# The first layer's output projection, second turn: seven products for eight, with the mixes on GpSimd and VectorE

## The reference

```python
o_p = sb_prompt(qkv[:, :, 0], qkv[:, :, 1], qkv[:, :, 2], sb_bias[i])
xp = xp + o_p.reshape(b, s, -1) @ w_o_a[i]
...
xs = xs + o_s.reshape(db, t, -1) @ w_o_a[i]
```

## Time and profile before

| | us |
|---|---|
| median of 3 executions | 1331.81 |
| lowest, highest | 1331.24, 1335.96 |
| the profiled execution | 1335.28 |
| its span | 1333.4 |
| TensorE busy | 1253.0 (94%) |
| VectorE busy | 629.5 (47%) |
| GpSimd busy | 495.7 (37%) |
| ScalarE busy | 404.2 (30%) |

### The profile page before, as it was taken

How to read it: one execution, slowest core, us unless ns; L and a number is a source line. 1 busy time by engine, 2 the same in 40 slices (tenths; PEclk the granted TensorE clock), 3 DMA queues, 4 the chain that set the end, 5 groups by cost and what they waited for, 6 DMA issues and landing times. The chain is left out here.

```text
span 1333.4 us, 21502 instructions
## 1 busy us (share of the span) xinstructions
PE 1253.0 (94%) x8796; PEld 881.1 (66%) x8796; DVE 629.5 (47%) x1026; ACT 404.2 (30%) x847; POOL 495.7 (37%) x415
## 2 busy tenths in 40 slices
PE   8999999999999998879999999999998989998887
PEld 6787887645666664436969868878756656664443
DVE  3478784623622221256357749648546562221123
ACT  2222422312122221155325526426015312221112
POOL 4456655100111111012986686686630101111102
PEclk8999999999999999999999999999998999999999
DMA  8446645477899999981111112013231899999998
GB/s 316 143 143 200 214 146 174 146 298 312 326 420 418 418 418 418 419 330 48 51 57 58 59 57 96 13 57 99 64 89 35 328 366 420 418 418 418 418 419 315
DMA packets 93317, 318.81 MB, mean 239 GB/s; under 512 B 32457, under 2 KB 44889, under 8 KB 68132
## 3 DMA queue, kind: packets, MB, share of 16 engines
q1 hardware_dynamic: 78500, 279.88, 54.2%
q0 software_dynamic: 13536, 33.29, 7.0%
q10 hardware_dynamic: 1184, 4.26, 0.8%
HBM read 300.06 MB, written 33.34 MB: 250 GB/s over the span
## 5 line engine op out<-in xcount | busy, mean ns | idle before, releaser
L1229 PE MATMUL ps<-slots,oT 128*64 128x256 f32 x1088 | 147.8, 384 | 18.7 <-DMA slots<-in_w_up 9.4
L1255 DVE TENSOR_TENSOR sg<-sg,ps 64x256 f32<-64x256 f32 x64 | 26.5, 413 | 236.3 <-ACT sg L1252 236.3
L1229 PEld LDWEIGHTS ps<-slots,oT 128*64 128x64 f32 x1088 | 100.5, 138 | 56.7 <-issue 18.1
L1756 POOL DMA_INDIRECT xs<-xn_rows,idx x30 | 30.8, 1026 | 235.5 <-PE ps L1218 177.0
L2136 PE MATMUL ps<-slots 128*128 128x384 f32 x320 | 107.2, 489 | 1.5 <-DVE vo L2534 1.5
L1252 ACT ACTIVATE sg<-ps 64x256 f32<-64x256 f32 x64 | 24.4, 381 | 231.4 <-PE ps L1229 231.4
L1762 POOL DMA_INDIRECT y_rows<-ysb,idx x30 | 30.2, 1008 | 166.8 <-DVE ysb L1264 162.3
L2136 PEld LDWEIGHTS ps<-slots 128*128 128x128 f32 x320 | 67.1, 214 | 34.4 <-issue 3.4
L1264 DVE COPY ysb<-ps 64x512 f32<-64x512 f32 x60 | 41.6, 694 | 85.8 <-PE ps L1247 81.1
L610 PE MATMUL ps<-xnT_a,wA 128*128 128x260 f32 (+1 forms) x320 | 77.0, 397 | 1.5 <-DVE xnT_a L874 1.4
L2457 ACT ACTIVATE slots<-slots,neg 128x128 f32<-128x128 f32 (+1 forms) x192 | 64.1, 417 | 43.3 <-DVE neg L2639 43.3
(11 more groups left out here) (384 smaller groups left out, 2664.0 us busy)
## 6 DMA issues: line engine op xcount, KB each, us to landing
slots<-in_w_gate SPq DMA_DIRECT2D x40, 1024.0 KB, 28.2
slots<-in_w_down SPq DMA_DIRECT2D x38, 1024.0 KB, 26.2
slots<-in_w_up SPq DMA_DIRECT2D x28, 1024.0 KB, 25.7
slots<-in_unit_weights_b SPq DMA_DIRECT2D x12, 1536.0 KB, 6.7
wA<-in_qkv_pairs_a SPq DMA_DIRECT2D x24, 512.0 KB, 3.3
spare<-in_w_up SPq DMA_DIRECT2D x12, 1024.0 KB, 29.2
apart<-in_w_gate SPq DMA_DIRECT2D x8, 1024.0 KB, 22.3
apart<-in_w_up SPq DMA_DIRECT2D x8, 1024.0 KB, 23.7
```

The lines of the kernel that those rows point to most:

```text
L1229: last = nc.tensor.matmul(bank(q)[lo:lo + CAP, 0:FE], x[:, k, :], wt[k], start=(k == 0), stop=(k == KT - 1))
```

## The change

Turn 1 is computed by a new class, `SevenProducts`, in place of 8 calls of `product` and `add`. The four tiles of tokens are two systems of two tiles each. In a system the pairs 0, 1 and 2, 3 are the two halves of the sum over pairs, and the two column halves of w_o the other side: a 2 x 2 by 2 x 2 block product, which Strassen's scheme does in 7 block products (table `SEVEN`) instead of 8. Its left operands are, for five of the seven, a sum or difference of two blocks of oT (`LEFT`, 128x256 each), its right operands, for five of the seven, a sum or difference of two blocks of w_o (`RIGHT`, 128x1024 each). Each product is added to or taken from one or two tiles of x. Pair 7 stays alone: its four tile products ride in products 3 and 4, which have one target, and in two products of their own, so a system has 9 products and 14 sums.

The five left mixes of a system are made by VectorE into `kv_tok`; those of the first system stand before its copies of the sample heads, those of the second between its sums. The five right mixes, which both systems use, are made once by GpSimd, behind its last mask, into `apart` (four) and qkvT (one). Banks 5, 6 and 7 are used in turn. The two expert pieces for `apart` are now issued when product 12 (the last that reads a right mix in apart) is done. ScalarE's squares wait for all sums of a system, and all stand behind its two copies of the sample rows; their junk buffer is now the one of the sample tokens' weights. `plan` and the counters keep the semaphores' counts for turns of any number of products and sums.

```diff
+        SEVEN = ((("s", 0), ("t", 0), ((0, 0, 1), (1, 1, 1))),
+                 ((0, 0), ("t", 1), ((0, 1, 1), (1, 1, 1))),
+                 ((1, 1), ("t", 2), ((0, 0, 1), (1, 0, 1))),
+                 (("s", 1), ("t", 3), ((1, 1, 1),)),
+                 (("s", 2), ("t", 4), ((0, 0, 1),)),
+                 (("s", 3), (0, 0), ((1, 0, 1), (1, 1, -1))),
+                 (("s", 4), (1, 1), ((0, 0, -1), (0, 1, 1))))
+        LEFT = (((0, 0), (1, 1), 1), ((1, 0), (0, 0), -1), ((0, 1), (1, 1), -1), ((1, 0), (1, 1), 1), ((0, 0), (0, 1), 1))
+        RIGHT = (((0, 0), (1, 1), 1), ((0, 1), (1, 1), -1), ((1, 0), (0, 0), -1), ((0, 0), (0, 1), 1), ((1, 0), (1, 1), 1))
...
+            def mix_left(self, dve, system, n):
+                if system:
+                    dve.wait_ge(self.proj.s_done, self.done([i for i, (a, _, _) in enumerate(SEVEN) if a == ("s", n)][0]))
+                (ta, ha), (tb, hb), sign = LEFT[n]
+                nc.vector.tensor_tensor(self.left[:, n], self.block(2 * system + ta, ha), self.block(2 * system + tb, hb),
+                                        ALU.add if sign > 0 else ALU.subtract).then_inc(self.s_left, 1)
+
+            def mix_right(self, eng, n, source):
+                (ha, na), (hb, nb), sign = RIGHT[n]
+                eng.tensor_tensor(self.right[n], source(ha, na), source(hb, nb), ALU.add if sign > 0 else ALU.subtract).then_inc(self.s_right, 1)
+
+            def product(self, pe, k):
+
+                system, i = k // self.per, k % self.per
+                out = bank(self.banks[k % len(self.banks)])
+                if k == 0:
+                    pe.wait_ge(self.proj.s_in[self.turn], 16 * len(self.proj.turns[self.turn]))
+                if k >= len(self.banks):
+                    pe.wait_ge(self.proj.s_added, self.added(k - len(self.banks)))
+                elif self.proj.added_before[self.turn]:
+                    pe.wait_ge(self.proj.s_added, self.proj.added_before[self.turn])
...
+                    for j in range(len(self.halves[0])):
+                        terms.append((self.left[:, a[1], j] if a[0] == "s" else self.tokens(self.halves[a[1]][j], 2 * system + a[0]),
+                                      self.right[b[1]][:, j] if b[0] == "t" else self.weights(self.halves[b[0]][j], b[1])))
+                if len(self.targets[i]) == 1:
+                    tile, n, _ = self.targets[i][0]
+                    terms += [(self.tokens(m, 2 * system + tile), self.weights(m, n)) for m in self.alone]
...
+            def add(self, dve, k):
+
+                system, i = k // self.per, k % self.per
+                dve.wait_ge(self.proj.s_done, self.done(k))
+                for j, (tile, n, sign) in enumerate(self.targets[i]):
+                    earlier = [e for e in range(i) for target in self.targets[e] if target[:2] == (tile, n)]
+                    if earlier:
+                        dve.wait_ge(self.proj.s_added, self.added(self.per * system + earlier[-1]))
...
                 load_first(sp, 0, range(NHOME))
+                sp.wait_ge(out_a.s_done, seven.done(seven.per + 3))
                 load_first(sp, 0, APART)
...
-                out_a.product(pe, 1, 0)
-                out_a.product(pe, 1, 1)
+                for k in range(4):
+                    seven.product(pe, k)
...
                 def square(t):
-                    act.wait_ge(out_a.s_added, out_a.added(t))
+                    act.wait_ge(out_a.s_added, seven.system_added(t // 2))
                     norm.square(act, t, junk)
 
-                square(0)
                 act.wait_ge(s_op, 1)
...
-                for t in range(1, NT - 2):
+                for t in range(NT - 2):
                     square(t)
...
+                dve.wait_ge(s_kvo, 64 * NPAIR)
+                for n in range(5):
+                    seven.mix_left(dve, 0, n)
                 for q in range(2):
                     dve.wait_ge(s_pv, q + 1)
...
+                pool.wait_ge(out_a.s_in[1], 16 * len(out_a.turns[1]))
+                pool.wait_ge(s_qk, 2 * NPAIR)
+                wo = flat(xnT)[:, 0:D * NPAIR // 2].rearrange("p (h k n) -> p h k n", h=2, k=2)
+                for n in range(5):
+                    seven.mix_right(nc.gpsimd, n, lambda half, cols: wo[:, half, :, 512 * cols:512 * cols + 512])
                 pool.drain()
                 for t in range(NT - 2):
                     norm.power(pool, t)
```

More of the change, by code:

```diff
@@ L282, in __init__, with plan @@
                 self.s_done, self.s_added = sem(f"oproj_done_{name}"), sem(f"x_added_{name}")
-                self.total = 2 * (NT - 1) * len(turns)
+                self.done_before, self.added_before = [0], [0]
+                for k in range(len(turns)):
+                    self.plan(k, 2 * (NT - 1), 2 * (NT - 1))
+            def plan(self, turn, products, sums):
+                del self.done_before[turn + 1:], self.added_before[turn + 1:]
+                self.done_before.append(self.done_before[turn] + products)
+                self.added_before.append(self.added_before[turn] + sums)
+                self.total = self.added_before[-1]
             def load(self, sp, turn, pairs):
@@ L290, in product @@
                 t, n = i // 2, i % 2
-                k, pairs = 2 * (NT - 1) * turn + i, self.turns[turn]
+                pairs, added = self.turns[turn], self.added_before[turn] + i - 1
                 if i == 0:
                     pe.wait_ge(self.s_in[turn], 16 * len(pairs))
-                if k >= 2:
-                    pe.wait_ge(self.s_added, k - 1)
+                if added > 0:
+                    pe.wait_ge(self.s_added, added)
                 for m in pairs:
@@ new lines, in build, with __init__, tokens, weights @@
+        LEFT = (((0, 0), (1, 1), 1), ((1, 0), (0, 0), -1), ((0, 1), (1, 1), -1), ((1, 0), (1, 1), 1), ((0, 0), (0, 1), 1))
+        RIGHT = (((0, 0), (1, 1), 1), ((0, 1), (1, 1), -1), ((1, 0), (0, 0), -1), ((0, 0), (0, 1), 1), ((1, 0), (1, 1), 1))
+        class SevenProducts:
+            def __init__(self, name, proj, turn, halves, alone, left, right, banks):
+                self.proj, self.turn, self.halves, self.alone, self.left, self.right, self.banks = proj, turn, halves, alone, left, right, banks
+                self.targets = [targets for _, _, targets in SEVEN] + ([((0, 1, 1),), ((1, 0, 1),)] if alone else [])
+                self.per = len(self.targets)
+                self.sums = sum(len(targets) for targets in self.targets)
+                self.s_left, self.s_right = sem(f"left_mixed_{name}"), sem(f"right_mixed_{name}")
+                proj.plan(turn, 2 * self.per, 2 * self.sums)
+            def tokens(self, m, tile):
+                return oT[:, m, 128 * tile:128 * tile + 128]
+            def weights(self, m, n):
+                return self.proj.w[m][:, 512 * n:512 * n + 512]
+            def block(self, tile, half):
+                ms = self.halves[half]
+                return oT[:, ms[0]:ms[-1] + 1, 128 * tile:128 * tile + 128]
+            def done(self, k):
+                return self.proj.done_before[self.turn] + k + 1
+            def added(self, k):
+                i = k % self.per
+                return self.proj.added_before[self.turn] + k // self.per * self.sums + sum(len(t) for t in self.targets[:i + 1])
+            def mix_left(self, dve, system, n):
[16 more added lines that the diff above has]
+                    pe.wait_ge(self.proj.s_added, self.proj.added_before[self.turn])
+                terms = []
+                if i < len(SEVEN):
+                    a, b, _ = SEVEN[i]
+                    if a[0] == "s":
+                        pe.wait_ge(self.s_left, len(LEFT) * system + a[1] + 1)
+                    if b[0] == "t":
+                        pe.wait_ge(self.s_right, b[1] + 1)
+                    for j in range(len(self.halves[0])):
[4 more added lines that the diff above has]
+                    terms += [(self.tokens(m, 2 * system + tile), self.weights(m, n)) for m in self.alone]
+                for j, (a, b) in enumerate(terms):
+                    last = nc.tensor.matmul(out, a, b, start=(j == 0), stop=(j == len(terms) - 1))
+                last.then_inc(self.proj.s_done, 1)
+            def add(self, dve, k):
[5 more added lines that the diff above has]
+                        dve.wait_ge(self.proj.s_added, self.added(self.per * system + earlier[-1]))
+                    elif self.proj.added_before[self.turn]:
+                        dve.wait_ge(self.proj.s_added, self.proj.added_before[self.turn])
+                    xh = x[:, 2 * system + tile, 512 * n:512 * n + 512]
+                    nc.vector.tensor_tensor(xh, xh, bank(self.banks[k % len(self.banks)]),
+                                            ALU.add if sign > 0 else ALU.subtract).then_inc(self.proj.s_added, 1)
+            def system_added(self, system):
+                return self.added(self.per * system + self.per - 1)
@@ L464, in build @@
```

(10 more changed lines are left out.)

23 lines of the change are left out of this document (14 added, 9 removed).

## The result

The changed kernel takes 1345.22 us (median of 4, 1343.31 to 1347.40), the kernel before 1331.76 (4 runs on the same chip); the ratio is 1.0093, 95% interval [1.0071, 1.0115]: **slower by some 12.4 us**. Forecast were 1335.7 and a range of 1330 to 1340.5. The profiled execution took 1343.31, span 1341.4.

A forecast was written before the change was run, and what follows sets the result against it. TensorE, busy 94% of the span, was taken as the bound. Products -3.43, tail +1.5 and taking turns +5.9 were summed as +3.9 us on the median 1331.81: forecast 1335.7, range 1330 to 1340.5.

The forecast's parts named there:

- Products: Second turn on TensorE: 36 matmuls instead of 40, -3.43 us, with no product stalled by a sum.
- Loads: Two apart pieces issued late, at about 321 us, still land before the boundary; cost 0.
- The shift: Experts' stage: its full DMA stream and all that follows move with the stage boundary at 328.68.
- Taking turns: First turn: GpSimd's right mixes and VectorE's SBUF instructions hold each other in turn, delaying TensorE's product 6 by +5.9 us.
- The first wait: First turn: TensorE waits for the first sum behind VectorE's held head 0 product, restarting +1.67 us later.
- The bound of 11: Upper bound of the taking-turns term, whose lower bound was 0 and whose taken value was 5.9 us.
- rival 3: First turn: GpSimd runs all five mixes without giving way and VectorE waits; +9.2 us, 1341.0, chance 0.08.
- Rivals 1 to 3: Mixes: 1, turns cost TensorE nothing (1329.9, chance 0.12); 2, only first 128x1279 product caught (1331.5, 0.10); 3, see rival 3.
- Tail: From second turn's last product to next stage: later sums +0.22, GpSimd's power +0.89, semaphore clearing 0.4; +1.5 us, bounds 1.1 and 1.9.
- what the change does to the time is what it does to the start of the next stage: Stage boundary at 328.68: everything behind it was taken to move by the same amount, with no further cost.
- The two terms that make TensorE wait: Taking turns in the first turn (+5.9 us) and the tail before the boundary (+1.5 us).

The follow-up runs named there:

- a_late: Changed kernel with GpSimd's right mixes begun only when VectorE's last 128x1279 product is done; 1342.01 us, ratio 1.0067.
- b_gap: Kernel before, with only the last square (tile 2) made to wait for all prompt sums; 1340.74 us, ratio 1.0073.
- b_gapbusy: b_gap with three matmuls that nobody reads in TensorE's idle time before the stage boundary; 1338.16 us, ratio 1.0032.
- a_tail: Changed kernel with products that end tile 0 put first and GpSimd's semaphore clearing before its last two powers; 1337.26 us, ratio 1.0034.
- a_busy: Changed kernel with three 128x512 matmuls on nothing at TensorE's end of the stage; 1344.05 us, ratio 1.0091.
- b_mixes: Kernel before plus only the five right mixes on GpSimd, read by nobody, with loads into apart waiting for them; 1340.0 us, ratio 1.0062.
- c_busy: c_so with one more matmul on nothing at TensorE's end of the stage; 1331.29 us, ratio 0.9989.
- a_half: Changed kernel with each right mix cut into two of 128x512; one execution at 1343.21 us.
- a_late_tt: a_late with VectorE's two-input sample-token instruction split into a one-input maximum and a two-input sum; one execution at 1342.11 us.
- c_so: a_tail with the right mixes begun only behind VectorE's last two-input instruction of the first turn; 1330.35 us, ratio 0.9989.

## Why the prediction was wrong

- **Products, right.** Forecast -3.43, measured -3.44, and no second-turn product waited for a sum.
- **Loads, right.** The apart pieces were issued at 319.26 and 319.63 (forecast about 321), and from the first expert matmul to the last expert's gates the time is the same to 0.1 us (to the next stage's first matmul 219.02 us, before 220.60). The shift is kept, also right.
- **Taking turns, right as a mechanism, short by 2.1 us in size.** Product 6 of the first turn started 6.2 us later against the turn's own start (forecast 5.9). The first wait grew by 1.97 (forecast 1.67); the slow product behind it cost nothing more, since product 6 waited for VectorE anyway. What was missing is the product behind the second wait, 4.50 instead of 2.84: 1.7 of the 2.1. With it the past values came 8.04 us later. The bound of 11 covered the total, but it was drawn from rival 3, not from the clock. Rivals 1 to 3 are out in the changed kernel: every two-input instruction beside the mixes was held, none over more than one mix at a time. In a_late, rival 3's mechanism did appear.
- **Tail, +1.5 forecast, +1.9 measured**, the upper bound. GpSimd's power comes 0.9 behind VectorE, as worked out; clearing 15 semaphores takes more than the 0.4 taken: from the power's end at 330.03 to 331.10 there are 1.07 us, and 0.33 of them also passed before, behind the last step (328.35 to 328.68), so about 0.7, an estimate. b_gap's trace gives the same (1.08 from the power's end to the boundary).
- **The step that failed: "what the change does to the time is what it does to the start of the next stage".** It held for the experts and not for what lies between, the routing. The two terms that make TensorE wait were priced at the length of the wait alone. The idle gap before the boundary grew from 0.46 to 2.36 us, the clock fell to 1.2 GHz, and routing took 38.07 us instead of 30.40: 7.7 us with no term, bound or rival. b_gap shows this alone (+7.4), b_gapbusy and a_tail take it away in their traces. With 7.7 and 1.7 for the clock the sum would have been 3.9 + 9.4 = 13.3. (The prediction's three terms as printed add up to 3.97, not 3.9; nothing hangs on it.)

The trace of before had the signs. TensorE's granted clock was 1.00 in the second turn and 0.94 at 540 to 570, where it is busy for 25.95 of 30 us: idle time and clock stood in one row. And the routing, which the prediction took as a stage that only shifts, had a short stretch at the low level of its own:

```profile
340.30:343.50 3.20, 3.20 (x14) 1.54 (x11) 2.79 (x15) 0.00 (x0) 0.00 (x0) 0.50 1.00 422
```

The Trainium skill ("TensorE: Matmul & The Clock Gate", section "Part 1: The HAM clock gate") says that the array's clock follows how busy TensorE has been recently; by that rule a gap can cost more than itself. The changed kernel and b_gap agree (7.7 and 7.4 us behind gaps of 2.36 and 2.09); the stretch just shown had no idle time of TensorE ahead of it since the boundary, so idle time is not all there is to it.

## What to carry to other kernels

Where a change lets TensorE stand idle, price the gap twice: its length, and what the stage behind it would lose if the clock falls; a stage of 30 us paid 7.7 us for 1.9 us more of gap. A saving of a few matmuls counts only if the chain behind the last of them (sum, square, power, clearing) is no longer than before, so order the products such that the last ones feed only the shortest chain. Before you give an "idle" GpSimd a row of long SBUF instructions, look at what VectorE does beside it and who waits for that.

## What the runs showed of the hardware that was not expected

- **Not every gap is followed by a fall, and not every fall has a gap ahead.** Idle gaps of TensorE of 0.46, 0.99 and 1.00 us before the boundary, and of 1.15 (a_busy) and 1.44 us in the first turn, left the clock up; those of 2.09, 2.32, 2.36, 2.45, 3.41 and 5.07 us were followed by a slower stretch. But in b_mixes the same place showed both:

```profile
260.62 4.48 PE L297 MATMUL ps<-wo_hi,oT 128*128 128x512 f32 x6 [3.47 <-DVE x L305]
...
271.36 2.84 PE L297 MATMUL ps<-wo_hi,oT 128*128 128x512 f32 x6 [2.59 <-DVE x L305]
```

  After 2.59 us idle the product kept its 2.84 us. In c_busy, with its gap before the boundary filled, the clock fell later in the routing, and routing took 33.9 us. Here a gap stood ahead again. The routing's eight records of fill (L228), which take 5.11 us in the kernel before with its low stretch in them, ran in 3.70; TensorE then waited 2.53 us for VectorE, and the fall came behind that:

```profile
333.08 3.70 PE L228 MATMUL ps<-cst 128*128 128x512 f32 x8
339.31 0.54 PE L1530 MATMUL ps<-scratch,cst 128*128 128x160 f32 x2 [2.53 <-DVE scratch L1708]
...
345.00:350.00 5.00, 5.00 (x44) 3.62 (x44) 1.92 (x8) 0.00 (x0) 1.07 (x1) 0.50 0.30 122
```

  And the kernel before was at 0.50 from 340.3 to 343.5 with no idle gap of TensorE in the timeline between the boundary (328.68) and then. So neither a gap nor its length alone decides; what does is not shown.
- **Who goes first at a hand-over between GpSimd and VectorE.** The Trainium skill ("SBUF — State Buffer", section "SBUF: two separate sides") says that whichever starts first has the shared ports for its whole instruction and the other blocks. Every hold here of an instruction with two inputs agrees, a_half's included. For a waiting instruction behind a row of GpSimd's, the runs show two patterns: in the changed kernel, b_mixes and a_half VectorE got in after one mix each time; in a_late (7.36 us for 0.42), a_late_tt (7.22, one input) and c_so (5.67 us for five left mixes, 1.75 in the changed kernel) it was held until the last mix was over. The kind of VectorE's instruction does not decide it, since a_late_tt's was held as well (one execution). Nor does its size alone: a_half's 128x256 got in ahead of GpSimd's last half mix (1.02 us for 0.42). What does stays open.
